# Stick-breaking attention on one NeuronCore: TensorE turns the weights of two groups back before, not after, the next group's scores

## The reference, cut to what matters

```python
z = jnp.einsum('bhqd,bhkd->bhqk', qi, k).astype(jnp.float32) * (d ** -0.5)
mask = (kpos[None, :] < tpos[:, None])[None, None]
log_beta = jax.nn.log_sigmoid(z)
log_one_minus = jnp.where(mask, jax.nn.log_sigmoid(-z), 0.0)
later = lax.cumsum(log_one_minus, axis=3, reverse=True) - log_one_minus
weights = jnp.where(mask, jnp.exp(log_beta + later), 0.0)
return jnp.einsum('bhqk,bhkd->bhqd', weights.astype(v.dtype), v)
```

## Time and profile before

| | |
|---|---|
| median of 3 runs | 1560.61 us (1558.74 to 1560.91) |
| the profiled execution's own time | 1560.53 us |
| its span, first to last instruction | 1558.7 us |
| busy over the span | PE 86%, PEld 57%, DVE 54%, ACT 37%, POOL 23% |
| mean granted TensorE clock | 0.946 of full speed |
| attention groups, from the first sigmoid to the last turn | about 548 to 785 us |

### The profile page before, as it was taken

How to read it: one execution, slowest core, us unless ns; L and a number is a source line. 1 busy time by engine, 2 the same in 40 slices (tenths; PEclk the granted TensorE clock), 3 DMA queues, 4 the chain that set the end, 5 groups by cost and what they waited for, 6 DMA issues and landing times.

```text
span 1558.7 us, 18280 instructions
## 1 busy us (share of the span) xinstructions
PE 1343.9 (86%) x6487; PEld 889.5 (57%) x6488; DVE 849.1 (54%) x1101; ACT 573.4 (37%) x736; POOL 365.1 (23%) x484
## 2 busy tenths in 40 slices
PE   5999999999999978888998992799999999999700
PEld 1433333466777745555644542688777888887600
DVE  5386874034531045666515566455888451548586
ACT  0200000124222156666602224145777442447453
POOL 0122310000410035656605441000000000000078
PEclk9999999999999999999999995799999999999955
DMA  9614131101021151212072315555999561539663
GB/s 345 235 54 162 55 130 39 54 1 66 3 75 43 48 166 35 49 33 51 26 286 95 122 61 202 202 216 215 355 384 385 221 228 55 221 136 381 241 226 114
DMA packets 138755, 234.43 MB, mean 150 GB/s; under 512 B 57320, under 2 KB 58928, under 8 KB 138696
## 3 DMA queue, kind: packets, MB, share of 16 engines
q1 hardware_dynamic: 128424, 196.39, 35.7%
q0 software_dynamic: 6496, 23.60, 4.4%
q10 hardware_dynamic: 3776, 13.67, 2.1%
HBM read 197.95 MB, written 35.68 MB: 150 GB/s over the span
## 4 chain that ended last, share of the span: by engine, by line
PE 66%; DVE 13%; ACT 7%; POOL 5%; issue 4%; DMA 2%; SPq 1%; ACTq 1%; POOLq 0%; DVEq 0%
PE psum L774 60%; DVE arena L1575 4%; DVE arena L1642 2%; PE psum L957 2%; ACT high L1353 2%; POOL arena L1973 1%; PE psum L1148 1%; DMA arena<-in_w_ada_mix 1%; ACT psum L1308 1%; POOL arena L1951 1%; ACT arena L1307 1%; POOL smalls L1967 1%; DVE arena L1576 1%; ACT a_high L1381 1%; PE psum L1154 1%
## 5 line engine op out<-in xcount | busy, mean ns | idle before, releaser
L774 PE MATMUL psum<-arena 128*64 128x128 f32 (+7 forms) x1524 | 256.6, 367 | 24.0 <-DVE arena L1642 11.6
L774 PEld LDWEIGHTS psum<-arena 128*64 128x64 f32 (+3 forms) x1524 | 131.9, 159 | 119.5 <-issue 90.6
L774 PE MATMUL psum<-win,hT 128*128 128x512 f32 (+1 forms) x432 | 193.0, 601 | 0.5 <-ACT hT L1192 0.5
L774 PE MATMUL psum<-high,h_high 128*128 128x512 f32 x416 | 164.9, 396 | 2.5 <-DVE h_low L1784 2.5
L774 PE MATMUL psum<-high,h_low 128*128 128x512 f32 x416 | 163.0, 392 | 0.0
L774 PEld LDWEIGHTS psum<-win,hT 128*128 128x128 f32 (+1 forms) x432 | 78.1, 185 | 110.8 <-issue 106.6
L1642 DVE TENSOR_TENSOR_SCAN arena<-psum,smalls 128x512 f32<-128x512 f32 (+4 forms) x68 | 66.3, 1014 | 91.7 <-ACT psum L1308 91.7
L1779 DVE TENSOR_TENSOR low_odd<-raw_odd,high 128x2048 fp32r<-128x2048 f32 x48 | 107.8, 2289 | 13.7 <-ACT high L1353 13.7
L1779 DVE TENSOR_TENSOR low_even<-raw_even,high 128x2048 fp32r<-128x2048 f32 x48 | 107.7, 2288 | 10.8 <-ACT high L1353 10.8
L1894 POOL TENSOR_TENSOR arena<-arena 128x512 f32<-128x512 f32 (+4 forms) x116 | 108.1, 931 | 9.3
L1938 POOL COPY smalls<-smalls 128x1 int32 x26 | 4.7, 182 | 421.1 <-PE psum L1148 415.2
(11 more groups left out here) (229 smaller groups left out, 2243.9 us busy)
## 6 DMA issues: line engine op xcount, KB each, us to landing
raw_even<-in_w_e_gate SPq DMA_DIRECT2D x8, 2048.0 KB, 10.6
raw_even<-in_w_e_up SPq DMA_DIRECT2D x8, 2048.0 KB, 16.6
raw_even<-in_w_e_down SPq DMA_DIRECT2D x8, 2048.0 KB, 14.8
raw_odd<-in_w_e_gate SPq DMA_DIRECT2D x8, 2048.0 KB, 10.4
raw_odd<-in_w_e_up SPq DMA_DIRECT2D x8, 2048.0 KB, 16.5
raw_odd<-in_w_e_down SPq DMA_DIRECT2D x8, 2048.0 KB, 15.0
win<-in_w_in SPq DMA_DIRECT2D x7, 2048.0 KB, 8.8
expert_rows<-arena ACTq DMA_DIRECT2D x26, 512.0 KB, 6.4
```

What stands on the lines that cost most here:

```text
L774: pe_last[0] = nc.tensor.matmul(*x, **y)
```

## The change

In every step of the attention loop PE issues `weights_turn(s - 2)` first and `qk(s + 1)` second. The list of entries that share `psum[2]` is as it was, since no scores are in it, and ACT's, DVE's, POOL's and SP's instructions stand as before.

```diff
             qk(0)
             for s in range(NG + 3):
+                if 2 <= s < NG + 2:
+                    weights_turn(s - 2)
                 if s + 1 < NG:
                     qk(s + 1)
-                if 2 <= s < NG + 2:
-                    weights_turn(s - 2)
                 if s >= 3:
                     values(s - 3)
```

## The result

| | before | after |
|---|---|---|
| median of 20 runs each | 1560.62 us (1556.32 to 1562.65) | 1563.07 us (1559.17 to 1573.57) |
| ratio, 95% interval | | 1.0022 [1.0012, 1.0033] |
| the profiled execution's own time, and its span | 1560.53, 1558.7 us | 1565.06, 1563.2 us |
| mean granted clock | 0.946 | 0.947 |

The forecast was 1560.0 us and "the same". The time lies in the forecast's range (1556 to 1564), but the kernel is slower, by just over the 0.2% that I had set as the bound; no difference at all lies outside the interval, 0.12 to 0.33%. The kernel of after was measured once more beside the experiments: 1563.94 us (11 runs), 1.0027 [1.0010, 1.0044].

A forecast was written before the change was run, and what follows sets the result against it. The prediction took PE to bound the attention, with only its idle 7.2 us a later pair to win. Its sum was 1560.5 + 0.7 (first pair) - 1.2 (three later pairs) = 1560.0 us, range 1556 to 1564.

The forecast's parts named there:

- Waits on PE 7.2, then 6.8: PE's summed waits in a later pair, before and after the change; a gain of 0.4 us a pair.
- step 3: Later pairs: the turning waits 0.9 us for DVE's copy of the preceding step's scales; no wait before.
- cache of step 4: Later pairs: the cache's turning waits 0.7 us for ACT's copy of weights; 0.41 before.
- step 5: Later pairs: the turning waits 1.4 us for copies of cache and sums; the scores waited 0.41 before.
- the waits did not vanish without new ones: Rival: later pairs' waits go and copies are in time, 19 us faster at most (1541), 1554 with a third; chance 0.17.
- the turning's wait did not simply add: Rival: ACT gains nothing, scores come 0.5 us later at four cache steps, 2 us a pair, 1567; chance 0.08.
- with PE busy for the same 47.2: Later pairs: PE's work stays 47.2 us, pairs take 53.5 to 54.6; nothing added or removed, same durations.
- -1.2 for three pairs: Later pairs: each gains 0.4 us from shorter PE waits, three of them 1.2 us.
- +0.7 (0 to 2): First pair: ends 0.7 us later through turnings waiting for ACT's retention copy; bounds 0 to 2 us.
- the waits mostly eat slack: First pair: turnings wait 0.3 to 0.9 us in eight wide steps, but ACT's chain is hardly longer.
- The rival with the clock: Rival: the clock falls once more in the first pair, up to 1563.4 us, two falls 1566.8; chance 0.13.
- a rival of 0.08: The rival in which the turning's wait simply adds, giving 1567 us; chance 0.08.

The follow-up runs named there:

- n1: Kernel before (old order) without the mask's bf16 products on the eight diagonal prompt groups a pair; 1577.51 us, one execution, not comparable with the others' times.
- n2: Changed kernel (new order) without the mask's bf16 products on the diagonal prompt groups; 1577.31 us, one execution, not comparable with the others' times.
- n3: Kernel before, scores still first, but with the values ahead of the weights' turning; 1593.89 us, measured once.
- a2: Kernel before with the new order only from step 17 on, that is in the later pairs; 1562.28 us, ratio 1.0016 to before.
- a1: Kernel before with the new order only in the first pair's steps (s < 17); 1563.5 us, ratio 1.0020 to before.
- a3: Kernel before with the new order only in steps whose preceding step ran no extra (cache, sums, scales, retention); 1563.5 us, ratio 1.0014 to before.
- b1: Changed kernel with extras ahead of the values in all pairs, except scales in steps that also turn cache; 1561.82 us, ratio 1.0012 to before.
- b3: Kernel before, but in the first pair's steps the turning goes first and the values go behind the extras; 1557.88 us, ratio 0.9983 to before.

## Why the prediction was right in its waits and wrong in its sign

**The waits of the later pairs: right.** "Waits on PE 7.2, then 6.8" measured 7.20 and 6.64. Step by step, forecast and seen in the third pair: scales of step 2, 1.1 and 1.00; step 3, 0.9 and 0.89; cache of step 4, 0.7 and 0.67; step 5, 1.4 and 1.46; step 7, 1.1 and 0.96; step 8, 0.4 and 0.43; step 9, 0.3 and 0.35; step 12, 0.9 and 0.90. The six waits for L1642 are gone, and the sigmoids follow the mask at once. So the carrying through by hand was sound, and two of the three rivals fall with it: the waits did not vanish without new ones, and the turning's wait did not simply add.

**The step that failed in the later pairs: "with PE busy for the same 47.2".** I held that "nothing is added or removed" and that the instructions keep their durations. The same instructions took 47.92. What changed is who follows whom: values behind the mask's bf16 products instead of a turning, 0.09 us more nine times. The forecast -0.4 us a pair turned into +0.16, and -1.2 for three pairs into +1.1: twice 0.16, and 0.8 in the fourth. That last one is a term that the sum did not have: I took the fourth pair as the others, and its last steps have no scores that the old order would put ahead of the turning. Without the mask the new order is 0.8 us a pair shorter (n1, n2), and n3 shows the dear neighbours with the scores unmoved. Why this pair of instructions costs more is open.

**The term that was mis-sized: "+0.7 (0 to 2)" for the first pair.** The place and mechanism were right: the turning waits behind L1315. Forecast were 0.3 to 0.9 us in eight steps, mostly as slack; measured were nine waits, six of 0.87 us and three of about 0.5. The pair grew by 0.92 us in the profile, but at a higher clock (0.92 against 0.90, 10.6 us at 1.2 GHz against 13.1). Against the old order at the clock of 0.92, in the profile of a2, it is 2.4 us longer, above my upper bound of 2; from the times, a1 gives about 1.9 (an estimate). What failed is "the waits mostly eat slack": of 6.7 us of new waits for L1315, and 2.9 more of turnings for DVE's copies, other waits gave back all but 2.2.

**The sum.** 1560.5 + 2.4 + 1.1 = 1564.0 at an equal clock, against 1563.07 and 1563.94 measured. By the times at equal clock it is less, 2.6 to 3.2 us (1563.0 and 1563.6 against 1560.4). The two agree to a microsecond; the clock's part is not known more closely than that.

**The rival with the clock.** "It decides if the mean clock in the first pair falls below 0.87": it was 0.92 in both profiles of the kernel after, and 1.00 in all its later pairs. So it did not decide this result. The rule of the Trainium skill, TensorE: Matmul & The Clock Gate, on a second HAM failure mode, had no effect in the kernel after, but four orders close to it had the clock fall in the second pair: a3, b1, a1 and a2. What differs is not more idle time (a3 has 1.5 us less of it a pair than before). The rule, which has short idle times bring the clock down, does not tell these orders apart; what does is open.

**The rule on banks.** The Trainium skill, Perfetto Trace Analysis, section Matmuls, that groups should rotate through banks so that the copying out of one overlaps the next, names what went wrong in the first pair; I gave it its full weight only in a rival of 0.08. Taken as a place to look it was right: b3 puts other work between the two writers and takes 3.3 us off that pair of the new order.

Left open: why the clock falls in later pairs of all the other orders but b3 and not in those of the kernel after; and why the values start later behind a bf16 product than a turning does.

## What to carry to other kernels

An instruction that moves changes what it follows and what follows it: list the neighbours on the bounding engine before and after, and where a pair of kinds is new to the trace, give it a price of either sign instead of "the same work". Where a queue in order has two writers of one bank in a row, the copy between them can be exposed whole, 0.87 us for 512 columns in six of nine places here; put work that needs neither behind the first. Work out the last steps of a loop by themselves, since they lack neighbours that the others have (0.8 us in the fourth pair here, 0.16 in the others). And for differences below half a per cent read the granted clock of all runs before you call an order better or worse: an order with fewer waits can lose by the clock what it wins.

## What the hardware showed that I had not expected

- A 64-column standing operand's fp32 product (values) starts 0.21 us after the bf16 pair of the mask started, a 128-column transpose 0.12 us after it; the same pair of bf16 products costs PE 0.6 us of busy time a pair of heads in one order and 1.8 in the other.
- Small reorderings of a TensorE queue change its time at 1.2 GHz by up to 12 us in 1560 (167 to 179), at the same work. Each such microsecond goes with 0.30 to 0.51 us of the kernel's time.
